# Weight halves interleaved column by column, and inputs read from the last column to the first

## The reference

```python
z_rec = h @ w_in[:, :REC_COLS]                                  # "rec"
z_rest = h @ w_in[:, REC_COLS:]                                 # "mix" and "merge"
merged = sigmoid(ga) * (y_a @ w_pa) + sigmoid(gb) * (y_b @ w_pb)    # "merge"
out = merged @ w_o                                              # "out"
(silu(a) * b) @ w_down,  a, b = split(h @ w_up)                 # "up", "down"
proj = einsum('btd,de->bte', u, w_in[l])                        # "attn"
y = einsum('bte,ed->btd', mixed, w_out[l])                      # "proj"
```

## Time and profile before

| | |
|---|---|
| median of 3 runs | 2324.36 us |
| span of the profiled execution | 2323.0 us |
| what lies around the span, taken as the difference | 1.4 us |
| PE busy, share of the span, matmuls | 2264.8 us, 97%, 18378 |
| PEld busy | 2180.9 us, 94% |
| DVE busy | 1633.6 us, 70% |
| ACT busy | 995.5 us, 43% |
| data moved | 475.6 MB, mean 205 GB/s |

### The profile page before, as it was taken

One profiled execution on the slowest core, in us unless ns is written; L12 is line 12 of the kernel. 1 busy time (PEld: TensorE's weight loads), 2 busy tenths in 40 slices (PEclk: granted clock), 3 DMA queues, 4 the chain that ended last, 5 costly groups with the idle time before them and its releaser, 6 DMA issues.

```text
span 2323.0 us, 48644 instructions
## 1 busy us (share of the span) xinstructions
PE 2264.8 (97%) x18378; PEld 2180.9 (94%) x18378; DVE 1633.6 (70%) x2515; ACT 995.5 (43%) x1402; POOL 8.4 (0%) x18
## 2 busy tenths in 40 slices
PE   5899999999999999989999999999999999999999
PEld 3678888999999999989999999999999999999999
DVE  4465564899976666988888887865557666667764
ACT  3322222555543434454444444444445444444452
POOL 0000000000000000000000000000000000000000
PEclk8999999999999999999999999999999999999999
DMA  9965455444356667975454555555556444444443
GB/s 406 389 252 218 181 223 210 164 145 144 144 217 236 258 236 287 344 306 197 181 181 181 185 187 188 185 198 180 184 192 217 156 153 147 160 146 161 146 179 128
DMA packets 69511, 475.62 MB, mean 205 GB/s; under 512 B 7728, under 2 KB 9776, under 8 KB 18384
## 3 DMA queue, kind: packets, MB, share of 16 engines
q1 hardware_dynamic: 68688, 467.59, 54.9%
q0 software_dynamic: 768, 7.26, 0.9%
HBM read 469.58 MB, written 5.24 MB: 204 GB/s over the span
## 4 chain that ended last, share of the span: by engine, by line
PE 88%; DVE 4%; ACT 1%; issue 1%; DVEq 0%; ACTq 0%
PE acc L795 83%; PE aux L795 4%; DVE lo L1157 1%; DVE ar L1384 0%; DVE qla L1377 0%; PE aux L1052 0%; ACT hi L462 0%; DVE raw L1167 0%; DVE qlb L1377 0%; DVE qs L1426 0%; DVE hxu L1174 0%; ACT n L666 0%; DVE n L1498 0%; ACT tt L594 0%; PE aux L887 0%
## 5 line engine op out<-in xcount | busy, mean ns | idle before, releaser
L1157 DVE TENSOR_TENSOR lo<-raw,hi 128x1024 fp32r<-128x1024 f32 (+1 forms) x716 | 811.9, 1167 | 196.8 <-ACT hi L462 192.2
L462 ACT ACTIVATE hi<-raw 128x1024 fp32r<-128x1024 f32 (+1 forms) x716 | 695.7, 1012 | 313.9 <-PE acc L795 259.9
L795 PE MATMUL acc<-hx,hi 128*128 128x256 f32 (+1 forms) x3072 | 662.7, 312 | 7.5 <-DVE lo L1157 4.1
L795 PEld LDWEIGHTS acc<-hx,hi 128*128 128x128 f32 x3072 | 496.1, 189 | 44.4 <-issue 6.9
L795 PE MATMUL acc<-hxu,hi 128*128 128x256 f32 x2816 | 502.7, 282 | 7.6 <-DVE hxu L1174 7.5
L795 PE MATMUL acc<-hx,lo 128*128 128x256 f32 (+1 forms) x1536 | 474.2, 309 | 0.0
L795 PEld LDWEIGHTS acc<-hxu,hi 128*128 128x128 f32 x2816 | 432.5, 189 | 8.8 <-issue 7.4
L795 PE MATMUL acc<-hxu,lo 128*128 128x256 f32 x1408 | 394.5, 280 | 0.0
L795 PE MATMUL acc<-u,hi 128*128 128x272 f32 (+1 forms) x2048 | 382.3, 287 | 0.0
L795 PEld LDWEIGHTS acc<-u,hi 128*128 128x128 f32 x2048 | 317.4, 188 | 4.5 <-issue 2.5
L795 PEld LDWEIGHTS acc<-hx,lo 128*128 128x128 f32 x1536 | 289.5, 189 | 17.5
(11 more groups left out here) (291 smaller groups left out, 2285.0 us busy)
## 6 DMA issues: line engine op xcount, KB each, us to landing
raw<-wts SPq DMA_DIRECT2D x390, 1024.0 KB, 4.8
raw<-wdown SPq DMA_DIRECT2D x64, 704.0 KB, 4.1
xc<-xct SPq DMA_DIRECT2D x1, 4096.0 KB, 12.3
rawx<-wts SPq DMA_DIRECT2D x2, 1024.0 KB, 24.7
x<-xct SPq DMA_DIRECT2D x1, 2048.0 KB, 9.8
park<-x POOLq DMA_DIRECT2D x1, 2048.0 KB, 10.4
xf<-park POOLq DMA_DIRECT2D x1, 2048.0 KB, 9.6
outt<-outs SPq DMA_DIRECT2D x16, 128.0 KB, 3.3
```

What stands on the lines that cost most here:

```text
L462: A.activation(HI[:, slot, a:b, 0:P], RAW[:, p % 4, a:b, :], ACT.Copy).then_inc(hi_half, 1)
L795: return pe.matmul(*a, **k)
L1157: V.tensor_tensor(LO[:, slot, a:b, 0:P], RAW[:, p % 4, a:b, :], HI[:, slot, a:b, 0:P].bitcast(F32), ALU.subtract).then_inc(lo_half, 1)
```

## The change

`HI` and `LO` become one tensor `HL`. A k-step is a block of 272 floats (`PAIR`, 1088 bytes, as much as a k-step of an input), in which HI's column n lies at place 2n and LO's at 2n+1. The 128 weights of a matmul are so 8 bytes apart and span 1024 bytes, and ScalarE and VectorE write, and VectorE reads, every second float. `HL` starts 64 bytes past a whole KB; the inputs start at whole ones. In `prod` the input and the output are both given with their columns reversed (`back`), so that the same sums go to the same places. `early` reads the new weights and keeps its column order.

`HL` takes the place where `RAWX` lay. `RAWX` becomes two tensors elsewhere, the second one over `SQ1`; its fetch waits for the last step of the sum of squares. A wait of VectorE, needed where `LO` lay over `RAWX`, goes.

```diff
-PW = P + 8
+PAIR = 2 * P + 16
+HLROW = 2 * 16 * PAIR - 16
-        HI = at("hi", 32, [P, 2, 16, PW], F32R)
-        LO = at("lo", 49, [P, 2, 16, PW], F32R)
+        HL = at("hl", 32 + 1 / 16, [P, HLROW], F32R)
-        RAWX = at("rawx", 49.5, [P, 2, 17, P])
+        RAWX = [at("rawx0", 193, [P, 16, P]), at("rawx1", 168, [P, 16, P])]
+        def half(slot, a, b, part):
+            first = (slot * 16 + a) * PAIR + part
+            return bass.AP(HL[:].tensor, first, [[HLROW, P], [PAIR, b - a], [2, P]])
+        def weights(slot, k, part):
+            first = (slot * 16 + k) * PAIR + part
+            return bass.AP(HL[:].tensor, first, [[HLROW, P], [2, P]])
...
             for s in range(2):
-                sp.dma_start(RAWX[:, s, 0:16, :], wts[UNIT0["rec"] + 2 * s]).then_inc(raw_early[s], 16)
+                if s:
+                    sp.wait_ge(sq1_read, 4)
+                sp.dma_start(RAWX[s][:], wts[UNIT0["rec"] + 2 * s]).then_inc(raw_early[s], 16)
...
-                    A.activation(HI[:, slot, a:b, 0:P], RAW[:, p % 4, a:b, :], ACT.Copy).then_inc(hi_half, 1)
+                    A.activation(half(slot, a, b, 0), RAW[:, p % 4, a:b, :], ACT.Copy).then_inc(hi_half, 1)
...
+            def back(t):
+                return t[:, :, ::-1] if len(t.shape) == 3 else t[:, ::-1]
...
-                        o = out(k)
-                        mm(o, HI[:, slot, k, 0:P], xh(k), start=first, stop=False)
-                        mm(o, HI[:, slot, k, 0:P], xl(k), start=False, stop=False)
-                        ins = mm(o, LO[:, slot, k, 0:P], xh(k), start=False, stop=last)
+                        o = back(out(k))
+                        mm(o, weights(slot, k, 0), back(xh(k)), start=first, stop=False)
+                        mm(o, weights(slot, k, 0), back(xl(k)), start=False, stop=False)
+                        ins = mm(o, weights(slot, k, 1), back(xh(k)), start=False, stop=last)
...
-                    V.tensor_tensor(LO[:, slot, a:b, 0:P], RAW[:, p % 4, a:b, :], HI[:, slot, a:b, 0:P].bitcast(F32),
+                    V.tensor_tensor(half(slot, a, b, 1), RAW[:, p % 4, a:b, :], half(slot, a, b, 0).bitcast(F32),
                                     ALU.subtract).then_inc(lo_half, 1)
...
-                        if h:
-                            dve.wait_ge(lo_half, 2 * i - 1)
```

More of the change, by code:

```diff
@@ L517, in _ @@
                     for a, b in ((0, 8), (8, 16)):
-                        A.activation(HI[:, i - 1, a:b, 0:P], RAWX[:, i - 1, a:b, :], ACT.Copy).then_inc(hi_half, 1)
+                        A.activation(half(i - 1, a, b, 0), RAWX[i - 1][:, a:b, :], ACT.Copy).then_inc(hi_half, 1)
             act.sem_inc(raw_full[0], 16)
@@ L851, in early @@
                     o = ACC[:, s, :].rearrange("p (s t) -> p s t", s=2)
-                    mm(o, HI[:, s, k, 0:P], xch(k), start=k == 0, stop=False)
-                    mm(o, HI[:, s, k, 0:P], xcl(k), start=False, stop=False)
-                    ins = mm(o, LO[:, s, k, 0:P], xch(k), start=False, stop=k == KD - 1)
+                    mm(o, weights(s, k, 0), xch(k), start=k == 0, stop=False)
+                    mm(o, weights(s, k, 0), xcl(k), start=False, stop=False)
+                    ins = mm(o, weights(s, k, 1), xch(k), start=False, stop=k == KD - 1)
                     if k == KD - 1:
@@ L1245, in _ @@
                         dve.wait_ge(hi_half, 2 * (i - 1) + h + 1)
-                        if h:
-                            dve.wait_ge(lo_half, 2 * i - 1)
-                        V.tensor_tensor(LO[:, i - 1, a:b, 0:P], RAWX[:, i - 1, a:b, :], HI[:, i - 1, a:b, 0:P].bitcast(F32),
+                        V.tensor_tensor(half(i - 1, a, b, 1), RAWX[i - 1][:, a:b, :], half(i - 1, a, b, 0).bitcast(F32),
                                         ALU.subtract).then_inc(lo_half, 1)
```

## The result

The changed kernel takes 2335.98 us (median of 4, 2335.0 to 2336.37) beside 2324.76 for the kernel before: a ratio of 1.0046, 95% interval 1.003 to 1.0062. It is slower by about 11 us, where 86 us less had been forecast.

The account below looks back on a forecast made before the run. TensorE, busy 97%, was taken as the bound. Matmul savings of 123.7 us less 5.4, 4.4, 19, 7.9 and 1.3 gave 85.7 us saved, so 2238.7 us; range 2190 to 2350.

Parts of the forecast that it names:

- the term 118.4 - 111.4 = 7.0 ns a matmul: 256-column matmuls: time drops from 118.4 ns to the 111.4 ns of a weight load once the streams never meet.
- The comparison with plain float32: Plain float32 durations fit 165 ns plus 0.83 a column with nothing lost; split products take 8 and 17 ns more.
- The excess that grows with columns: Time above the columns: 11.7 ns with 256 columns, 12.7 with 272, 20 with 512, so not all a fixed price.
- the fourth case: Nothing changes: the excess belongs to the matmul itself and layout is nothing, 2325.7 us; chance 0.09.
- The prediction's own sign of a wrong mechanism: Mechanism wrong if "rec", whose loads are beside half a matmul only, gains per matmul no more than "up".
- The direction of loading and a constant phase: Weights load from last column to first, so reversed inputs run beside them at a fixed 64 bytes and never meet.
- A distance there may be a bad one: In "down" and "attn" the streams' distance differs, so half of both stages' savings was counted, -19 us.
- The wide products: 512-column matmuls in "rec": 233 to 218 ns, 15.8 us saved, half of it taken off for the row change, -7.9.
- Splits: VectorE and ScalarE writing every second float, VectorE also reading so: cost 0; at the upper end 1.22 to 2.1 us each.
- Start: Second early unit's fetch waits for the last sum of squares, delaying the modulation stage: 1.3 us, between 0 and 3.
- The bad place: Both streams stay together at a bad distance or cross more often: 285 ns for every matmul, 2406 us; chance 0.22.
- The case of VectorE as the bound: Writes at every second float cost 0.56 us a split, so VectorE limits "up", "mix" and "out": 2302 us; chance 0.13.

## Why the prediction was wrong

**The step that failed** is the conclusion drawn from the earlier trace rows, "that a matmul loses time where its inputs and the weights being loaded beside it meet", and with it the term 118.4 - 111.4 = 7.0 ns a matmul (8 and 15 for the wider ones), 123.7 us in sum. The rows had shown a swing of a few nanoseconds that has to do with addresses. I took them as proof of the cause of the whole excess. The runs take the 118.3 ns apart:

| part of a 256-column matmul | ns | from |
|---|---|---|
| columns, 256 / 2.4 | 106.7 | granted clock 1.00 |
| fixed | 2.5 | inputs still, short loads: 109.2 |
| inputs that move | 7.9 | ordinary inputs, short loads: 117.1 |
| full loads beside them | 1.2 | 118.3 in "up" before; 117.4 in "mix" before; reversed 117.6 to 119.6 by distance, forward 118.2 to 120.6 |

Only the last row is the meeting of streams, and as far as the run with still weights shows it, another 1 ns of the row above: with the weights standing still a matmul took 116.1 ns, with short loads 117.1. So a better layout had some 2.2 ns to give, not 7. The change gave nothing in "up" (118.3 both), took 0.9 ns in "mix", and took 1.6 and 1.2 in "attn".

The first three rows also give the wide products, which they were not made from: 512 / 2.4 + 2.5 + 2 x 7.9 = 231.6 ns as an estimate, and 231.7 were measured forward, 232.4 before. With 192 columns the same sum gives 88.4 for 88.9 measured, with 128 59.8 for 61.1.

- **The comparison with plain float32** (165 ns + 0.83 a column) was the false support. I read the missing excess there as streams at one rate that don't meet. The half rate asks half as much of the inputs' path per ns, which explains it equally. That is argued: no run let the inputs of a plain float32 product stand still, and none shows what in the inputs' path costs the 7.9 ns.
- **The excess that grows with columns** was seen ("20 more" with 512) and spoke for the fourth case, as the prediction itself said: one load lies beside only half of a wide matmul. That was the clue to weigh; it had 0.09. The prediction's own sign of a wrong mechanism, that "rec" gains no more per matmul than "up", came too: "rec" lost 0.7 ns, "up" gained none.
- **The direction of loading and a constant phase** were right in kind: reversed is 1.3 to 1.8 ns better than forward in "up" and 1.1 ns over the four distances of "down", though 1.1 worse in "attn" of the changed kernel, and the repetition over 8 k-steps went.
- **"A distance there may be a bad one"** for "down" and "attn" was right for "attn": at distance 0 it lost 4.9 us. But it had been counted as half of a gain, not as a loss.
- **The wide products** were taken to gain 15 ns each. Reversed, they lose 0.7 ns (232.4 to 233.1): 1056 x 0.7 = 0.7 us, most of the 1.0 us that the lag grows by through them.
- **Narrow products outside "up"** were all priced at 118.4 ns before. "Mix" stood at 117.4 and "down" at 117.7, so that even the gain to 111.4 would have been smaller there by some 3 us together.
- **Splits** at 0: right for VectorE (1219 for 1218 ns), and so its rival as the bound fell away. For ScalarE the cost of 0.13 us a split was within "hides the like". The rule of 16-byte lines in the Trainium skill ("Advanced Engine Details and Errata", "Memory Cachelines") holds for VectorE's writes; ScalarE's writes (1182 for 1052 ns), and TensorE's inputs at every second float (229 for 117 ns), have two hits in a line and pay. There the measurement decides.
- **Start**: 1.3 us forecast within 0 to 3, 2.3 measured with the wait alone.
- **The rivals.** The bad place asked for 285 ns in every matmul and 2406 us; in its mild end, one stage at the wrong distance, it is part of what happened. The fourth case, "the excess belongs to the matmul itself", was nearest to the true cause with its 2325.7 us: it lacks another 3 us at the start, "mix" and "attn". The case of VectorE as the bound counted 16 us for "rec", where the prediction's own sum leaves 15.8 + 2.7 - 7.9 = 10.6. The rule that TensorE waits for nobody (the Trainium skill, "SBUF — State Buffer", "Who interferes with whom") would have given the better forecast. It is not quite what was measured: layout moves a reversed matmul by 2 ns between the best and the worst distance seen, not by none, but not by 7.

The 10.1 us between the two traces are: the start 4.3, of which the wait is 2.3 and the DMAs' lower rate about 2; shorter waits at the start of "rec" -1.5; the wide products 1.0; "mix" 1.4; "attn" 4.9. The medians differ by 11.2, 1 us more, where single times of the kernel before lie as much as 6 us apart (2323.56 to 2329.43). Two causes stay open: that of the lower rate, and why the old layout has 117.4 ns in "mix" and 118.3 in "up".

## What to carry to other kernels

A pattern in the durations proves that something modulates them, not that it makes up their mean: before a layout is built on it, let one stream stand still (a step of 0, or half the weights) in one stage and read the count in a window. Here that single run puts the ceiling near 2.2 ns of 118.3, where the prediction had counted 7.0. And when addresses matter at the level of 1%, the distance has to be chosen for each stage: it cost "attn" 4.9 us at one distance and gave 5.2 back at another, and the wide matmuls wanted the opposite direction. Nor does one stage stand for the others: the price of a matmul before the change has to be read in each.

## What the runs showed of the hardware

- Full-rate float32 matmuls, beside weight loads of 64 columns, took 109.2 ns for 256 columns with an input that stands still, 117.1 with one that moves and 229.1 with every second float. Sixteen floats taken 16 times took 120.7.
- A weight load of 128 columns is a floor of 111.4 to 112 ns a matmul: 192 columns took no less (112.0).
- Weights at a step of 8 bytes load in 196 ns for 188 (recorded durations of one load, below: after, then before), and matmuls beside them took as little as 117.6 ns. Whether the floor of 111.4 rises with that step, no run shows.
- With interleaved weights and reversed inputs, matmuls in "down" took 119.6, 118.3, 117.6 and 118.2 ns at distances of 0, 64, 128 and 192 bytes between weights and inputs, modulo 256.
- Writes at every second float: VectorE 0, ScalarE 0.13 us for 1024.

```profile
L807 PEld LDWEIGHTS acc<-u,hl 128*128 128x128 f32 x3072 | 382.7, 196 | 4.3 <-issue 2.5 <-DVE skf L1651 0.4
```

```profile
L795 PEld LDWEIGHTS acc<-u,hi 128*128 128x128 f32 x2048 | 317.4, 188 | 4.5 <-issue 2.5 <-DVE skf L1637 0.4
```
